# Weight halves made one unit later, and first turned rows one unit later, in the second part of attention

## The reference

```python
h = rms_norm(x, ln_attn_g[i])
dq, dk, dv, mq, mk, mv = jnp.split(h @ w_in[i], cuts, axis=-1)
# dq, dk, mq, mk get an rms_norm over each group of 64 columns
# diff attention: per head two softmaxes p0, p1;  a = p0 - lam * p1;  out = rms_norm(a @ v) * (1 - lam_init)
# moba attention: at 256 rows one block, so plain causal attention, 8 heads
x = x + jnp.concatenate([y_diff, y_moba], axis=-1) @ w_out[i]
x = x + conv_ffn(rms_norm(x, ln_ffn_g[i]), w_up[i], conv_w[i], conv_b[i], w_down[i])
```

## Time and profile before

| | us |
|---|---|
| median of 3 runs | 2143.45 (2141.76 to 2145.78) |
| the profiled execution | 2143.34 |
| its span | 2141.5 |
| outside the span | 1.8 |

### The profile page before, as it was taken

How to read it: one execution, slowest core, us unless ns; L and a number is a source line. 1 busy time by engine, 2 the same in 40 slices (tenths; PEclk the granted TensorE clock), 3 DMA queues, 4 the chain that set the end, 5 groups by cost and what they waited for, 6 DMA issues and landing times.

```text
span 2141.5 us, 31502 instructions
## 1 busy us (share of the span) xinstructions
PE 2082.7 (97%) x12146; PEld 1794.8 (84%) x12146; DVE 1342.7 (63%) x2333; ACT 962.3 (45%) x1602; POOL 133.6 (6%) x140
## 2 busy tenths in 40 slices
PE   8999999999999999999999999999999999999998
PEld 6779998778999888888888788888877899888997
DVE  6756667667777227558445556868473588575565
ACT  4545555554555325352332453232344464445443
POOL 1001000000110100000100001111110000100100
PEclk9999999999999999999999999999999999999999
DMA  8336655424555321212222104424323234241543
GB/s 261 139 129 242 226 210 191 158 99 163 182 177 177 124 99 60 74 65 75 74 89 96 52 31 168 179 108 157 131 79 131 98 119 138 104 171 59 187 159 128
DMA packets 78811, 284.23 MB, mean 133 GB/s; under 512 B 8758, under 2 KB 9666, under 8 KB 78664
## 3 DMA queue, kind: packets, MB, share of 16 engines
q1 hardware_dynamic: 70560, 256.15, 34.2%
q10 hardware_dynamic: 6072, 18.73, 2.4%
q0 software_dynamic: 2032, 7.35, 1.2%
HBM read 276.35 MB, written 5.83 MB: 132 GB/s over the span
## 4 chain that ended last, share of the span: by engine, by line
PE 68%; DVE 8%; ACT 5%; issue 2%; POOL 0%; DMA 0%; DVEq 0%; ACTq 0%
PE pb L947 13%; PE pb L949 13%; PE pb L948 13%; PE pb L960 5%; PE pb L961 5%; PE pb L962 5%; DVE SPL L1951 2%; PE pb L966 2%; ACT SPH L1403 2%; PE pb L1282 2%; PE pb L1179 2%; PE pb L1263 2%; PE pb L1105 1%; PE pb L1107 1%; PE pb L1106 1%
## 5 line engine op out<-in xcount | busy, mean ns | idle before, releaser
L1951 DVE TENSOR_TENSOR SPL<-RAW,SPH 128x1024 fp32r<-128x1024 f32 x462 | 562.0, 1231 | 413.1 <-ACT SPH L1403 402.3
L947 PE MATMUL pb<-HTH,SPH 128*128 128x256 f32 (+1 forms) x2008 | 649.2, 323 | 9.7 <-POOL HTL L2559 2.3
L949 PE MATMUL pb<-HTH,SPL 128*128 128x256 f32 (+1 forms) x2008 | 639.0, 318 | 0.0
L948 PE MATMUL pb<-HTL,SPH 128*128 128x256 f32 (+1 forms) x2008 | 638.8, 318 | 0.0
L1403 ACT ACTIVATE SPH<-RAW 128x1024 fp32r<-128x1024 f32 x462 | 476.8, 1048 | 245.2 <-PE pb L949 119.5
L947 PEld LDWEIGHTS pb<-HTH,SPH 128*128 128x128 f32 x2008 | 383.8, 191 | 42.6 <-issue 6.4
L948 PEld LDWEIGHTS pb<-HTL,SPH 128*128 128x128 f32 x2008 | 384.0, 191 | 26.3
L949 PEld LDWEIGHTS pb<-HTH,SPL 128*128 128x128 f32 x2008 | 383.8, 191 | 26.2
L960 PE MATMUL pb<-SPH,HTH 128*128 128x512 f32 x640 | 255.3, 399 | 2.5 <-ACT GV L1601 2.0
L962 PE MATMUL pb<-SPL,HTH 128*128 128x512 f32 x640 | 250.6, 392 | 0.0
L961 PE MATMUL pb<-SPH,HTL 128*128 128x512 f32 x640 | 250.4, 391 | 0.0
(11 more groups left out here) (272 smaller groups left out, 2495.3 us busy)
## 6 DMA issues: line engine op xcount, KB each, us to landing
RAW<-in_w_up SPq DMA_DIRECT2D x88, 512.0 KB, 4.4
RAW<-in_wa SPq DMA_DIRECT2D x64, 512.0 KB, 3.3
RAW<-in_w_in SPq DMA_DIRECT2D x48, 512.0 KB, 4.4
RAW<-in_wmg SPq DMA_DIRECT2D x48, 512.0 KB, 3.3
RAW<-in_wbr SPq DMA_DIRECT2D x48, 512.0 KB, 3.2
RAW<-in_w_down SPq DMA_DIRECT2D x44, 512.0 KB, 4.7
RAW<-in_w_ada SPq DMA_DIRECT2D x24, 512.0 KB, 4.8
ARAW<-in_w_ada ACTq DMA_DIRECT2D x24, 512.0 KB, 4.2
```

Of the source, the lines that this page charges most:

```text
L947: T.matmul(o, wh[:, kt, :], xh[:, kt, n0:n1], start=kt == 0, stop=False)
L948: T.matmul(o, wh[:, kt, :], xl[:, kt, n0:n1], start=False, stop=False)
L949: m = T.matmul(o, wl[:, kt, :], xh[:, kt, n0:n1], start=False, stop=kt == 7)
L1951: W.tensor_tensor(lo, raw, hi.bitcast(F32), SUB).then_inc(*dve.tick(s["lo_dve"], ("u", u)))
```

## The change

- Behind unit n = 20 of the input product, `late` is set and stays so until the eight `w_out` units are done. While it is set, `get_w` reaches only two units ahead and not three. The third is added inside the head step, behind scores, probs and y, and before turn and values. Units 24 to 30 are so made one place later; unit 31, which has no head step behind it, is made before the next unit.
- The first unit of `w_up` behind attention (36) is no longer split before the last `w_out` unit, but behind `res1` and `stats`.
- `y_turn` 0 stands behind unit 23 and before head step 9, no longer behind unit 22 and head step 8.

No instruction is added or removed. The order in which banks 4 and 5 are given out stays as it was.

```diff
--- before.py
+++ after.py
@@ -36,7 +36,7 @@
 EARLY = 3
 FIRST = 11
 BESIDE = (11, 12, 14, 15, 17, 18, 20, 21, 22, 23)
-EARLY_Y = 22
+EARLY_Y = 23
 BEHIND = ((0, 0), (0, 1, 0), (0, 0), (0, 2, 0, 0), (3,), (), (), ())
 LEAD = ((6, 1), (1, 1))
 BO = (4, 4, 4)
@@ -138,7 +138,7 @@
         self.loads = self.splits = self.nsplit = self.gets = 0
         self.held, self.loaded, self.ready, self.off_raw = set(), set(), {}, set()
         self.slots, self.raw_before, self.slot_before = [None] * NS, {}, {}
-        self.split_on, self.limit = [0], 1 << 30
+        self.split_on, self.limit, self.late = [0], 1 << 30, False
         self.run()
 
     def add(self, *step):
@@ -196,7 +196,7 @@
         self.gets += 1
         if self.order is not None:
             assert self.order[u] == (name, idx, cols, kind)
-            self.split_upto(min(u + NS + 1, self.limit))
+            self.split_upto(min(u + NS - 2 if self.late else u + NS + 1, self.limit))
         return u
 
     def put_w(self, u):
@@ -353,6 +353,8 @@
                 self.add("y", l, ends[2])
                 self.give(ends)
                 ends = None
+            if self.late:
+                self.split_upto(self.gets + NS - 2)
             if u - LT in turned:
                 n = self.take((4, 5), ("tr", l, u - LT))
                 self.add("turn", l, u - LT)
@@ -403,10 +405,12 @@
                 if l == 0:
                     self.add("mask")
                 self.add("mark", f"attn{l}")
+            if n == BESIDE[-4]:
+                self.late = True
+            if n == EARLY_Y:
+                self.y_turn(l, 0)
             if n in BESIDE:
                 next(heads)
-            if n == EARLY_Y:
-                self.y_turn(l, 0)
         out = [self.group_n(("wo", l, g), f"w_out{l}", g, (0, 1), LO4, ("Y", l)) for g in range(2)]
         for unit in range(4):
             for g in range(2):
@@ -421,6 +425,7 @@
                     else:
                         next(heads)
         drain(heads)
+        self.late = False
         self.norm_filled(f"f{l}", (7,))
         self.ada_ring = (3,)
         for t in range(2):
```

## The result

The changed kernel takes 2153.42 us (median of 16 runs, 2148.56 to 2158.0), the kernel before, run beside it, 2145.88 (16 runs, 2140.45 to 2150.06). The ratio is 1.0035, with an interval of 1.0026 to 1.0044: 7.5 us slower, 5.6 to 9.4. The forecast was 5.8 us.

What follows compares the result with a forecast made beforehand. TensorE, busy in 97% of the span, was taken as the bound, paced in attention by DVE's and ACT's head steps. 2.59 + 0.31 = 2.90 us per layer, 5.8 in both, on 2143.34 gave 2149.1 us; range 2145.0 to 2153.0.

Steps and rivals of the forecast that it cites:

- Steps 1 to 4: Attention, y_turn 0 to turn 13: replayed queues make turn 7 0.34 us late, turn 9 0.74, turn 11 1.73, turn 13 2.59.
- The slow stretch: From turn 11 to scores 14, TensorE at the lower clock of 1.2 GHz: 1.63 us per layer, taken as unchanged.
- Step 4: At turn 13, behind hi 29 and the copy of turn 12: 2.59 us late per layer, 128.42 against 125.83.
- a longer slow stretch: Rival, slower: the low clock in attention lasts twice as long, another 1.63 us per layer, 2152.4 us; chance 0.12.
- part of the slow stretch would lie on idle time: In attention, clock falls at the same time, so 117.8 to 119.2 costs nothing: -0.7 us per layer, 2147.7 us.
- Step 5: Unit 36, before the FFN: lo 36 takes 1.13 us on DVE, 0.31 per layer reaches TensorE; bounds 0 and 1.13.
- It wins: Rival, faster: halves fit idle time, waits at y_turn 0 and y_turn 1 go; -4.5 us per layer, 2134.3; chance 0.08.
- The loads bite: Rival, slower, at the FFN: lo 36 costs 1.13 us in full, load 41 equally late; 3.9 us, 2153.0; chance 0.04.
- No slow stretch: Rival, same: the clock might not fall in attention, 1.63 us less per layer, leaving 1.27, 2145.9 us; chance 0.18.

## Why the prediction was right or wrong

**The order of the queues: right.** Steps 1 to 4 of the replay gave seven times; the first five are within 0.1 us. Each wait that it named is there, within 0.2 us of its length: 1.4 forecast and 1.51 measured at turn 7; 0.9, 1.5 and 0.8 against 0.91, 1.34 and 0.70 at y_turn 1, scores 13 and turn 11; 0.85 and 0.78 at turn 13. With TensorE kept busy in both orders they are 5.8 us apart, the forecast's size; that it fits to the tenth is luck, with an interval of 2.8 either way. That moving lo 28 back gives less than moving lo 27 takes, and that hi 28 and lo 28 hold up scores 13 and turn 11, is what the kernels with unit 27 back and with the high halves back show.

**The slow stretch: mis-sized.** Step 4 put scores 14 "with a slow stretch of the same cost", and this term of the sum failed. Its price was 1.63 us in the earlier trace rows and is 6.80 - 3.90 = 2.90 in layer 0; in layer 1 turn 11 to scores 14 takes 6.34 against 3.90 with TensorE kept busy, 2.44:

```profile
472.16 0.90 PE L971 MATMUL pb<-IDENT,E 128*128 128x128 f32 x3
...
478.50 0.49 PE L1057 MATMUL pb<-QKT 64*128 64x128 f32 x2
```

That is 1.3 and 0.8 us over the forecast. The rival of a longer slow stretch, which I gave 0.12, is the one that came true, in part. I had the idle times that speak for it (3.2 us against 2.0) and took the old cost all the same. Its counterpart, that part of the slow stretch would lie on idle time, shows in layer 1 alone, where the clock is down from about 470.5 and the wait of 0.70 at turn 11 is gone, and it took off only 0.5 us. What sets the length of a slow stretch stays open: it follows idle time, but the same waits were followed by a long or a short one (unit 27 back), by a short one or none (the kernel with three low halves late), in two layers of one execution.

**The norm before the FFN.** Step 5 gave 0.31 per layer. Between the end of the fill and the first FFN matmul, layer 1 grew by 0.24 (8.20 late at its start, 8.44 at its end), as forecast; layer 0 by 0.74, with the clock down in part of it, where it was 1.00 before; no term of the sum had this:

```profile
152.00:154.00 2.00, 1.06 (x7) 1.00 (x7) 1.86 (x7) 1.06 (x1) 0.00 (x0) 0.78 0.95 367
154.00:156.00 2.00, 2.00 (x11) 2.00 (x11) 2.00 (x5) 1.21 (x3) 0.00 (x0) 0.50 1.02 401
```

So the sum is 5.8 for order and norm as forecast, about 2.1 for the longer slow stretches of attention, and 0.4 for this one: 8.3, against 8.0 seen at 510.43. The timed 7.5 (5.6 to 9.4) holds both the forecast 5.8 and this.

**The absolute time.** 2153.42 lies above the range's 2153.0. Of the distance of 4.3 to 2149.1, 1.7 are the change (7.5 against 5.8); 2.5 are that the kernel before has its median of 16 runs at 2145.88, while I started from one execution of 2143.34 (and three runs with a median of 2143.45). Either miss alone would have left the time inside the range (2143.34 + 7.5 = 2150.9; 2145.88 + 5.8 = 2151.7). The starting point is a matter of the clock as well: of the 63 runs of the kernel before beside the experiments, the seven with a mean granted clock of 0.994 took 2141.4 to 2143.1 us, the seventeen with 0.990 took 2145.1 to 2147.2, and the three with 0.988 took 2149.4 to 2149.9. The execution that I started from had 0.994. I had taken it for exact; this spread should have widened the range.

**The rivals.** "It wins" was wrong for this edit, but it named the right condition, that ACT is done with the high halves in time: once they stay early, 5.4 to 7.7 us are won against the 9 that it named. The waits at y_turn 0 and y_turn 1 go or shrink to some 0.2, those of 0.39 and 0.44 behind y_turn 1 stay, and turn 7 gets one of 0.4 to 1.6. "The loads bite" was put at 0.04 and didn't come true in the changed kernel (ACT waits 1.71 us for the load of unit 37, 1.77 before); that something like it is close by is shown by unit 36 alone back, where the load of that unit comes late and the kernel is 4.7 us slower. "No slow stretch" came true, in the changed order, only where TensorE was kept busy, and there only behind turn 11.

## What to carry to other kernels

When work is moved later in a list that several engines share, replay each engine's queue by itself: a step that helps on one (the low halves on DVE) can stand in the way on another (the high halves on ACT), and the two can be moved apart. Look first at what reads out the bank that TensorE waits for, and put nothing ahead of that read-out. Count waits of about a microsecond twice, once for themselves and once for the slower matmuls that may follow; and where the kernel before pays this too, only the growth of it is the change's. Start a forecast from the median of many runs, and look at the granted clock of the one that was profiled.

## What had not been expected of the hardware

The lower clock costs about as much as the short waits ahead of it. In layer 0 of the changed kernel TensorE at 1.2 GHz, behind waits of 0.91, 1.34 and 0.70 us, lost 2.9 us, as much as these waits together. Fourteen repeated matmuls of 0.11 us in each layer, which compute nothing new, win 5.4 us in the changed kernel, and nine in each layer win 3.6 us in the kernel before. Of the difference between the two kernels it is the smaller part, some 1.7 of 7.5 us.

Whether and how long the clock falls isn't fixed by the waits. Behind 0.22, 0.39 and 0.44 us it fell in layer 1 of one kernel (5.54 us from turn 11 to scores 14) and stayed up in layer 0 of the same execution (3.92); behind 1.5 us at turn 7 it fell in one layer of the kept-busy kernel and in neither of the changed one. With it the time of one and the same kernel moves: the kernel before took 2141.4 to 2149.9 us in the runs beside the experiments, the faster the higher its mean granted clock.
